# Start, one level of the mixer and the last token tile of a two-block network, in another order

## What is computed

```python
def rms_norm(x, g):
    xf = x.astype(jnp.float32)
    y = xf * lax.rsqrt(jnp.mean(xf * xf, axis=-1, keepdims=True) + EPS)
    return (y * g.astype(jnp.float32)).astype(x.dtype)
...
    for l in range(DEPTH):
        x = x + 0.5 * rms_norm(swiglu_ffn(rms_norm(x, norm_pre[l, 0]), ffn1_w_in[l], ffn1_w_out[l]),
                               norm_post[l, 0])
        mixed = token_mixer(rms_norm(x, norm_pre[l, 1]), w_mix_in[l], ...)
        x = x + rms_norm(mixed, norm_post[l, 1])
        ...
# hgrn2_chunkwise, one chunk
        decay = jnp.exp(jnp.where(causal, rel, -jnp.inf))
        scores = jnp.sum(qc[:, :, :, None, :] * kc[:, :, None, :, :] * decay, axis=-1)
        o = o_inter + jnp.einsum("bhts,bhsv->bhtv", scores, vc)
...
# second block, the last step of each layer
        x = layer_norm(alpha * x + conv_ffn(x, ffn_w_up[layer], ffn_conv_w[layer],
                                            ffn_conv_b[layer], ffn_w_down[layer]),
                       ln_ffn_g[layer], ln_ffn_b[layer])
```

## Time and profile before

| | us |
|---|---|
| median of 3 runs | 2421.17 |
| lowest and highest | 2420.96, 2421.32 |
| the profiled execution | 2421.15 |
| its span, first to last instruction | 2419.4 |
| busy PE in the span | 2396.1 |
| mean granted clock of PE, share of full | 0.996 |

### The profile page before, as it was taken

One profiled execution on the slowest core, in us unless ns is written; L12 is line 12 of the kernel. 1 busy time (PEld: TensorE's weight loads), 2 busy tenths in 40 slices (PEclk: granted clock), 3 DMA queues, 4 the chain that ended last, 5 costly groups with the idle time before them and its releaser, 6 DMA issues.

```text
span 2419.4 us, 27040 instructions
## 1 busy us (share of the span) xinstructions
PE 2396.1 (99%) x12164; PEld 2034.0 (84%) x12164; DVE 1092.4 (45%) x1036; ACT 806.9 (33%) x891; POOL 65.1 (3%) x39
## 2 busy tenths in 40 slices
PE   9999999999999999999999999999999999999998
PEld 8888889888888888898987888888888977888887
DVE  4333225565553332255735644423535546544424
ACT  4232224454542232233432433321322432433311
POOL 0000000230100000000000000000000000000000
PEclk9999999999999999999999999999999999999999
DMA  4232323211133232242421322321422511232321
GB/s 162 87 105 90 120 87 120 79 38 70 48 110 105 87 105 98 85 162 88 159 85 35 122 104 88 105 105 70 157 93 82 192 70 70 88 105 88 121 94 63
DMA packets 34405, 238.30 MB, mean 98 GB/s; under 512 B 3949, under 2 KB 4333, under 8 KB 6514
## 3 DMA queue, kind: packets, MB, share of 16 engines
q1 hardware_dynamic: 34288, 236.56, 27.3%
q10 hardware_dynamic: 2, 0.00, 0.0%
HBM read 234.46 MB, written 2.10 MB: 98 GB/s over the span
## 4 chain that ended last, share of the span: by engine, by line
PE 97%; ACT 1%; DVE 1%; DMA 1%; issue 0%
PE bank L444 54%; PE bank L518 28%; PE bank L850 4%; PE bank L483 4%; PE bank L506 1%; PE bank L877 1%; PE bank L704 1%; PE bank L897 1%; DMA raw<-w_full 1%; PE bank L636 0%; ACT w_hi L1020 0%; PE bank L646 0%; PE bank L587 0%; PE bank L605 0%; PE bank L888 0%
## 5 line engine op out<-in xcount | busy, mean ns | idle before, releaser
L444 PE MATMUL bank<-a_hi,w_hi 128*128 128x512 f32 (+1 forms) x2112 | 785.5, 372 | 0.6 <-DVE a_lo L1546 0.6
L444 PE MATMUL bank<-a_lo,w_hi 128*128 128x512 f32 (+1 forms) x2112 | 781.0, 370 | 0.0
L444 PE MATMUL bank<-a_hi,w_lo 128*128 128x512 f32 (+1 forms) x2112 | 781.0, 370 | 0.0
L1497 DVE TENSOR_TENSOR w_lo<-raw,w_hi 128x2048 fp32r<-128x2048 f32 x207 | 476.4, 2302 | 504.3 <-ACT w_hi L1020 503.4
L1020 ACT ACTIVATE w_hi<-raw 128x2048 fp32r<-128x2048 f32 x207 | 394.4, 1906 | 367.5 <-DMA raw<-w_full 367.5
L444 PEld LDWEIGHTS bank<-a_hi,w_hi 128*128 128x128 f32 x2112 | 398.0, 188 | 69.7 <-issue 1.7
L444 PEld LDWEIGHTS bank<-a_lo,w_hi 128*128 128x128 f32 x2112 | 397.9, 188 | 67.7
L444 PEld LDWEIGHTS bank<-a_hi,w_lo 128*128 128x128 f32 x2112 | 398.1, 188 | 67.5 <-issue 0.7
L518 PE MATMUL bank<-w_hi,h_hi 128*128 128x512 f32 x704 | 274.5, 390 | 0.2 <-DVE w_lo L1497 0.2
L518 PE MATMUL bank<-w_hi,h_lo 128*128 128x512 f32 x704 | 274.0, 389 | 0.0
L518 PE MATMUL bank<-w_lo,h_hi 128*128 128x512 f32 x704 | 273.9, 389 | 0.0
(11 more groups left out here) (284 smaller groups left out, 2317.1 us busy)
## 6 DMA issues: line engine op xcount, KB each, us to landing
raw<-w_full SPq DMA_DIRECT2D x207, 1024.0 KB, 4.7
rows_ab<-rows SPq DMA_DIRECT2D x8, 1024.0 KB, 5.3
x<-x SPq DMA_DIRECT2D x4, 512.0 KB, 5.7
mem_raw<-mem SPq DMA_DIRECT2D x2, 1024.0 KB, 8.2
out<-x SPq DMA_DIRECT2D x4, 512.0 KB, 2.6
raw<-w_full SPq DMA_DIRECT2D x2, 512.0 KB, 5.7
ab_rows<-ab_rows SPq DMA_DIRECT2D x1, 768.0 KB, 7.6
wg_raw<-w_gates SPq DMA_DIRECT2D x1, 512.0 KB, 5.8
```

The costliest lines, as they stand in the source:

```text
L444: last = mm(bank[:, b + m, cols], w[:, s, c0:c0 + P], act_in[:, k, cols], start=(k == 0 and j == 0), stop=(k == KD - 1 and j == 2))
L1497: V.tensor_tensor(w_lo[:, u % SLOTS, :], raw[:, u % SLOTS, :], w_hi[:, u % SLOTS, :], ALU.subtract).then_inc(w_split, 1)
```

## The change

Five edits:

- The first gain is loaded as a column layout of 128 partitions by 8 (`gain0`). DVE multiplies it into eight scaled identity matrices (`diag0`, one instruction on 1024 columns), and PE spreads it with eight full products of `ones` by `diag0` (16 passes) in the place of two products of one row. The constant products now use `ones` alone, and stand as 6 ahead of the gain products, 3 behind them, 1 behind the turn of tile 0 and 9 behind the turn of tile 1 (before: 14, 6 and 8).
- At the start ACT copies the half unit before it takes tile 0, and DVE subtracts it before the low part of tile 0.
- ACT's `split_upto(mi + 12)` moves behind `level_exp(6)`, `q_decay` and `mlstm_v(0)`. In the mixer's output product `part(1, 3)` moves ahead of the turn of tile 0 and `part(2, 3)` ahead of the turn of tile 1.
- The last token tile of the last stage is computed, normed and stored in two halves of 512 columns (`last_tile`, `last_ln`).
- `mem_hi`, `mem_lo`, `k_mem`, the norm rows and some small tiles lie 192 to 320 bytes later, and everything from `x` on 512 bytes later.

```diff
-        X0 = 107 * KB - 512
+        X0 = 107 * KB
...
-        row0 = at("row0", [1, D], f32, X0 + 80 * KB)
...
-        rows_ab = arena("rows_ab", [P, 2, D], f32, 88.0625)
-        ln_u = arena("ln_u", [P, 2, D], f32, 96.0625)
+        rows_ab = arena("rows_ab", [P, 2, D], f32, 88.3125)
+        ln_u = arena("ln_u", [P, 2, D], f32, 96.3125)
...
+        gain0 = arena("gain0", [P, KD], f32, 88)
+        diag0 = arena("diag0", [P, KD, P], f32, 92)
...
-        mem_hi = arena("mem_hi", [P, KD, MEM], f32r, 64)
-        mem_lo = arena("mem_lo", [P, KD, MEM], f32r, 72)
-        k_mem = arena("k_mem", [P, KD, MEM], f32, 80)
+        mem_hi = arena("mem_hi", [P, KD, MEM], f32r, 64.3125)
+        mem_lo = arena("mem_lo", [P, KD, MEM], f32r, 72.3125)
+        k_mem = arena("k_mem", [P, KD, MEM], f32, 80.3125)
...
-            for t in range(NT):
+            for t in range(NT - 1):
                 sp.wait_ge(x_final, t + 1)
                 sp.dma_start(a["out"][t], x[:, t, :]).then_inc(out_s, 16)
-            sp.wait_ge(out_s, 16 * NT)
+            for half in range(2):
+                cols = slice(half * T, (half + 1) * T)
+                sp.wait_ge(x_final, NT + half)
+                sp.dma_start(a["out"][NT - 1, :, cols], x[:, NT - 1, cols]).then_inc(out_s, 16)
+            sp.wait_ge(out_s, 16 * (NT + 1))
...
+            def last_tile(name):
+
+                n, t = UNITS[name], NT - 1
+                for half in range(2):
+                    for u in range(n - 3, n):
+                        s = (U0[name] + u) % SLOTS
+                        for r in range(2):
+                            for j, (w, act_in) in enumerate(((w_hi, h_hi), (w_lo, h_hi), (w_hi, h_lo))):
+                                c0 = r * D + half * T
+                                last = mm(bank[:, 2 * t + half, :], act_in[:, 2 * u + r, tok(t)], w[:, s, c0:c0 + T],
+                                          start=False, stop=(u == n - 1 and r == 1 and j == 2))
+                    last.then_inc(half_done if half == 0 else y_done, 1)
...
-                    mm(bank[:, 4, 0:P], ident[:, :], ones[:, :], start=True, stop=True)
+                    mm(bank[:, 4, 0:P], ones[:, :], ones[:, :], start=True, stop=True)
...
+                part(1, 3).then_inc(out_used, 1)
                 turn("mixout", 0)
-                part(1, 3).then_inc(out_used, 1)
+                part(2, 3).then_inc(out_used, 1)
                 turn("mixout", 1)
-                part(2, 3).then_inc(out_used, 1)
                 part(3, 3).then_inc(y_done, 1)
...
-            pe.wait_ge(ident_in, 16)
-            pe.wait_ge(row0_in, 16)
-            for n in range(2):
-                last = mm(bank[:, 6 + n, :], ones[0:1, :], row0[:, n * T:(n + 1) * T], start=True, stop=True)
+            warm(6)
+            pe.wait_ge(diag0_made, 1)
+            for k in range(KD):
+                last = mm(pair(6)[:, k, :], ones[:, :], diag0[:, k, :], start=True, stop=True)
             last.then_inc(gain_mm, 1)
-            warm(14)
+            warm(3)
             turn("start", 0)
-            warm(6)
+            warm(1)
             turn("start", 1)
-            warm(8)
+            warm(9)
...
-            act.dma_start(row0[:, :], a["first_gain"]).then_inc(row0_in, 16)
+            act.dma_start(gain0[:, :], a["first_gain"]).then_inc(gain0_in, 16)
...
-            take_turned("start", 0)
             act.wait_ge(half_loaded, 16)
             S.activation(w_hi[:, 0, 0:FULL // 2], raw[:, 0, 0:FULL // 2], ACT.Copy).then_inc(half_hi, 1)
+            take_turned("start", 0)
             take_turned("start", 1)
...
-            split_upto(mi + 12)
             level_exp(6)
             S.activation(q_dec[:, :, :], Gc[:, :, :], ACT.Exp).then_inc(SIG["q_decay"], 1)
             mlstm_v(0)
+            split_upto(mi + 12)
...
+            def last_ln(name):
+
+                t = NT - 1
+                halves = slice(0, T), slice(T, D)
+                for n, cols in enumerate(halves):
+                    dve.wait_ge(*((y_done, Y0[name] + NT) if n else (half_done, 1)))
+                    link(V.scalar_tensor_tensor(x[:, t, cols], x[:, t, cols], ALPHA, bank[:, 2 * t + n, :], ALU.mult, ALU.add))
+                    ins = V.bn_stats(bnl[:, t, 6 * n:6 * n + 6], x[:, t, cols])
+                link(ins)
+                V.bn_aggr(stat[:, t, 0:2], bnl[:, t, :]).then_inc(ln_var, 1)
+                dve.wait_ge(ln_var, LN0[name] + t + 1)
+                for cols in halves:
+                    ins = V.scalar_tensor_tensor(ln_u[:, t % 2, cols], x[:, t, cols], stat[:, t, 0:1], rows_ab[:, 0, cols],
+                                                 ALU.subtract, ALU.mult)
+                link(ins)
+                dve.wait_ge(ln_sd, LN0[name] + t + 1)
+                link(V.reciprocal(stat[:, t, 3:4], stat[:, t, 2:3]))
+                for cols in halves:
+                    V.scalar_tensor_tensor(x[:, t, cols], ln_u[:, t % 2, cols], stat[:, t, 3:4], rows_ab[:, 1, cols],
+                                           ALU.mult, ALU.add).then_inc(x_final, 1)
...
+            dve.wait_ge(ident_in, 16)
+            dve.wait_ge(gain0_in, 16)
+            V.tensor_tensor(diag0[:, :, :], ident[:, :].unsqueeze(1).broadcast_to([P, KD, P]),
+                            gain0[:, :].unsqueeze(2).broadcast_to([P, KD, P]), ALU.mult).then_inc(diag0_made, 1)
             dve.wait_ge(gain_mm, 1)
             norm_rms("start", 0)
             norm_rms("start", 1)
-            low_turned("start", 0)
             dve.wait_ge(half_hi, 1)
             V.tensor_tensor(w_lo[:, 0, 0:FULL // 2], raw[:, 0, 0:FULL // 2], w_hi[:, 0, 0:FULL // 2],
                             ALU.subtract).then_inc(half_split, 1)
+            low_turned("start", 0)
             low_turned("start", 1)
```

More of the change, by code:

```diff
@@ L133, in build @@
         row_em = arena("row_em", [HEADS, T], f32, 94.0625)
-        masks = arena("masks", [P, 8, P], u32, 96.0625)
-        gbias = arena("gbias", [P, 2], f32, 100.0625)
-        ct = arena("ct", [P, 2, NT, HEADS], f32, 100.125)
-        mcol = arena("mcol", [P, 4, NT], f32, 100.25)
-        hcol = arena("hcol", [P, NT, HEADS], f32, 100.3125)
-        g_end = arena("g_end", [P, HEADS * NT], f32, 100.375)
-        mtmp = arena("mtmp", [P, T], f32, 100.5)
-        row_nm = arena("row_nm", [HEADS, T], f32, 102.5)
-        sel = arena("sel", [HEADS, HEADS, P], f32, 104.5)
+        masks = arena("masks", [P, 8, P], u32, 96.3125)
+        gbias = arena("gbias", [P, 2], f32, 100.3125)
+        ct = arena("ct", [P, 2, NT, HEADS], f32, 100.375)
+        mcol = arena("mcol", [P, 4, NT], f32, 100.5)
+        hcol = arena("hcol", [P, NT, HEADS], f32, 100.5625)
+        g_end = arena("g_end", [P, HEADS * NT], f32, 100.625)
+        mtmp = arena("mtmp", [P, T], f32, 100.6875)
+        row_nm = arena("row_nm", [HEADS, T], f32, 102.6875)
+        sel = arena("sel", [HEADS, HEADS, P], f32, 104.6875)
         hgate = arena("hgate", [P, HEADS, T], f32, 24)
@@ L197, in build @@
         consts_v = sem("consts_v")
-        row0_in = sem("row0_in")
+        gain0_in = sem("gain0_in")
+        diag0_made = sem("diag0_made")
         gain_mm = sem("gain_mm")
@@ L212, in build @@
         x_final = sem("x_final")
+        half_done = sem("half_done")
         turned = sem("turned")
@@ L536, in down @@
                 pe.wait_ge(h_done, F0[f] + KF)
-                for t in range(NT):
+                for t in range(NT - (name == "down3")):
                     last = part(n - 3, t)
@@ L546, in down @@
                     part(n - 1, t).then_inc(y_done, 1)
+                if name == "down3":
+                    last_tile(name)
+            def last_tile(name):
[9 more added lines that the diff above has]
+                    last.then_inc(half_done if half == 0 else y_done, 1)
             def mix_out(name):
@@ L1603, in ln_out @@
                 if name == "down3":
-                    for t in (2, 3):
-                        add_ln(name, t)
-                        norm_ln(name, t)
+                    add_ln(name, 2)
+                    norm_ln(name, 2)
+                    last_ln(name)
                     return
@@ L2091 @@
         "vectors": np.concatenate([vector(i[n]) for n, _ in VECTORS], axis=1),
-        "first_gain": pre[0][None],
+        "first_gain": vector(pre[0]),
         "rows": np.stack([every(np.stack([np.asarray(g), np.asarray(b)])) for g, b in gains]),
```

## The result

| | before | after |
|---|---|---|
| median of the runs, us | 2421.07 (2419.53 to 2421.32, 4 runs) | 2402.36 (2400.74 to 2402.46, 4 runs) |
| profiled execution: time, span | 2421.15, 2419.4 | 2402.46, 2400.6 |
| predicted | | 2404.4, range 2403.0 to 2409.0 |

The ratio after to before is 0.9922 [0.9905, 0.9940]. The sign was right and the size nearly so; the range left out a part of the change that I had put at nothing.

A forecast was written before the change was run, and what follows sets the result against it. PE was busy 2396.1 of 2419.4 us, so gains must come from its 23 us standing still or its slow time. Terms 9.7 + 4.2 + 1.5 + 1.4 = 16.8 off 2421.15 gave 2404.4, range 2403.0 to 2409.0.

The forecast's parts named there:

- Level split: Mixer: moving ACT's copy behind the exponential gains 9.7 us: 4.25 of gap, 3.54 and 1.94 of low clock.
- Start: Kernel start: real products begin at 13.5 in the place of 17.70, gaining 4.2 us (cases from 1.1 to 4.9).
- Rival B: Start: the clock is low when the head begins, costing 2.1 us in all, 2406.5; chance 0.15.
- Mixer's output: Turns at the mixer's output: PE's idle 1.49 goes, gaining 1.5 us, bounds 0.5 and 1.5.
- Last tile: Kernel end: DVE ends 1.1 us sooner and the smaller last store saves 0.3; 1.4 in all (1.0 to 1.8).
- The other offset: Tiles moved to new addresses: gains nothing, bounds 0 on both sides but for slower passes.
- case D: All PE passes: new addresses cost time; 1.4 ns each over 12164 passes uses up the gain; chance 0.03.
- B's dearer case: Start: the low clock at the head lasts as long as in the mixer, costing 5.0 us in all, 2409.4.

The follow-up runs named there:

- experiment 6: The changed kernel with its whole start put back (one-row gain products, old constant products, old ACT and DVE order): 2405.37 us.
- experiment 4: The changed kernel with ACT's copy of unit mi + 12 put back ahead of the last level's exponential: 2409.90 us.
- experiment 2: The changed kernel with all weights and the constants moved 192 bytes further on: 2429.31 us.
- experiment 1: The changed kernel with only mem_hi, mem_lo and k_mem put back to their old offsets: 2404.46 us.
- experiment 7: The changed kernel with only the gain put back to one-row products, the rest of the new start kept: 2402.67 us.
- experiment 9: The changed kernel with only the last tile put back to whole rows and one store of 512 KB: 2403.00 us.

## Why the prediction was right and wrong, point by point

- **Level split.** 9.7 predicted, 9.73 in the profile, 9.4 by itself on the kernel before. The three terms (gap, two stretches of low clock) are the right ones. The cover was 3.4 by the sum; `take_scores(7)` waited for PE, as it was to, and ended at 537.33, 3.3 ahead of the piece's end.
- **Start.** 4.2 predicted, 4.04. `gain0` let DVE begin at 2.84 (I had 2.7), the gain products began at 4.12 (4.0) and ended at 7.2 (7.0), turn 0 stood at 8.81 (8.4 to 9.5 for its whole), the head at 13.66 (13.5). The clock rose at about 6.5, as predicted. In the nine other profiles of the same start the 16 gain passes took 2.19 to 3.34 (3.11 here), and the head stood at 13.07 to 13.96. That the gain came out at 4.04 is in part luck: the profile of before was a late one (experiment 6), and against a head at 16.8 the same start gains 2.8 to 3.7.
- **Rival B** (low clock at the head), 0.15: the turns are at 1.09 and the 18 passes at 0.11. The clock did fall at another place, in the mLSTM part, which B did not speak of. The Trainium skill (TensorE: Matmul & The Clock Gate, Part 4: PE-mode transpose) says that transposes don't engage the full clock; that spoke for B. In this trace the two turns of the start, 1.09 each with one constant product between them, did not pull it down. Where the clock did fall, at 587, a turn of 0.60 stood ahead, but so did 3.5 us of products over few rows, and in the five profiles where the clock fell behind head 0 only these stood ahead and no turn. So the rule is neither shown nor refuted there.
- **Mixer's output.** 1.5 predicted, 1.48 in the rows as a remainder, and 1.4 of wait come back when it is undone.
- **Last tile.** 1.4 predicted, 1.54, with both terms off against each other: DVE's part gained 0.85 (I had 1.1), the store 0.69 (I took 0.3, bound 0.7). The store was mis-sized by the thought that the other half would still be moving; the profile's own issue lines have 2.0 us to landing for 256 KB and 2.6 for 512 KB. The Trainium skill's estimate, 0.6 less (DMA: Bandwidth & Descriptors, Anatomy of one DMA), agrees with them in the difference; with it the store's term would have been nearer. In the whole it does not: an estimate by the same page is 2.6 and 3.2 us, and its section is on DMAs issued by GpSimd, where SP issues these.
- **The other offset.** "Nothing ... bounds 0 on both sides but for case D" is **the step that failed**. It gained 3.26 us. The argument was that products on tiles at different places cost the same and that DVE takes 1.22 at both ends. But those tiles are a whole multiple of 512 bytes away from the weights, and the memory tiles were too; with everything from `x` on moved by 512 and the memory by 320, the memory's distance became one that no row of before shows. DVE's duration says nothing of PE's. I had the mechanism in rival D, with a price in ns for each product, and gave it one sign only. The trace of before had a bound for both signs: 48 products over 256 columns took 5.82 on line 483 and 5.75 on line 850, 1.5 ns apart for each, or 1.1 us over the memory's 768. Even that would have been small: half of the 768 gained 2.0 ns each, the other half 6.5.
- **Not in any case:** the low clock at 587, -1.57. The two profiles with the gap (before and experiment 4) do not have it; of the ten without the gap and with the same order of small products seven have it and three do not, so that removing the gap brings it on is not shown. Without it the time would have been 2400.9, where the quicker executions are.

The sum: 16.8 predicted; the same four terms measured 4.04 + 9.73 + 1.48 + 1.54 = 16.79. The miss is 3.26 - 1.57 and 0.3 unplaced. So close an agreement is partly luck: a start of 4.04 against a late execution, and a last tile whose two terms were off against each other. Two bounds of the prediction do not fit its own terms: the low ones together are 9.7 + 1.1 + 0.5 + 1.0 = 12.3, so 2408.9 and not 2408, and B's dearer case, 2409.4, lies outside the range that was to hold B. Neither touches the miss, which is at the lower end.

## What to carry to other kernels

An edit that "only moves a tile" is a term of the sum with a bound on both sides: the price per product (here 2.0 and 6.5 ns) times the number of products that read it, and the sign wasn't known from the rows of before. A wait that PE shows costs more than its length wherever the half clock follows it: here 4.25 of gap and 5.5 behind it, for one line in ACT's order. Before constant products are put in to hold the clock, look whether the real ones ahead of them are over few rows: here full products with a diagonal in them did the same work, and the clock was up at about 6.5 and not at about 12.

## What the runs showed of the hardware

- The pace of a product in the rounded format depends on how far apart the tiles that PE reads lie. In ns for each product, by how much further on the weights lie against the other tile than before (the common move of 512 bytes left out):

| products | as before | 192 bytes | 384 bytes |
|---|---|---|---|
| 256 columns, weights loaded, the other tile streamed | 119.8 (memory, 5.75 over 48) | 117.7 (memory, 5.65) and 117.9 (line 452, 5.66) | 118.5 to 120.0 (memory, 5.69 to 5.76) |
| 256 columns, weights streamed | 119.9 (memory, 23.03 over 192) and 120.8 (line 491, 5.80 over 48) | 113.4 (memory, 21.78) and 115.0 (line 491, 5.52 over 48) | 118.7 (memory, 22.79 over 192) |
| 512 columns, weights loaded (line 452) | 226.9 (10.89 over 48) | 229.0 (10.99) | not tried |
| 512 columns, weights streamed (line 526) | 226.7 | 233.3 | not tried |

 The same distance gives about the same pace on two different pairs of tiles. Which rule lies behind it stays open, and why the two widths go opposite ways. The distance of a product's own two tiles is not all of it: of the three products of a set on line 452 over 512 columns, experiment 2 slows the two with `w_hi` (means of 394 and 393 ns, 391 and 389 in experiment 1) and leaves the one with `w_lo` at 389, though `w_lo` was moved as well.
- Two products of one row (four passes), 3.78 us of busy PE, left the clock low by the lengths of the passes behind them: the rise came at about 12, with full products in their place at about 6.5.
- The clock can fall while PE is busy throughout. In eight profiles it fell for 3 to 4 us, each time right behind the same small products (4 rows, then 64 rows), behind head 0 in five and behind a later head in three; in the profiles of the kernel before and of experiments 2, 4, 7 and 9, with the same order of products there, it did not. With the two kinds apart for all four heads the one profile shows none, and the five times speak against it. Why one execution has it and the next not was not found.
